# Three projection units opened by token halves at the norm borders, all norm sums in two banks, a fourth unit's weights in a home of their own

## The reference

```python
def rmsnorm(x, g):
    return x * rsqrt(mean(x * x) + EPS) * g

def swiglu(h, w_gu, w_down):
    gate, up = split(h @ w_gu, 2)
    return (silu(gate) * up) @ w_down

for l in range(2):
    h = rmsnorm(x, norm_pre[l, 0])
    x = x + 0.5 * rmsnorm(swiglu(h, ffn1_gu[l], ffn1_down[l]), norm_post[l, 0])
    h = rmsnorm(x, norm_pre[l, 1])
    mix = concat(attention, short_conv, recurrence)      # all from h @ w_in[l]
    x = x + rmsnorm(mix @ w_out[l], norm_post[l, 1])
    h = rmsnorm(x, norm_pre[l, 2])
    x = x + rmsnorm(memory_attention(h, mem[l]), norm_post[l, 2])
    h = rmsnorm(x, norm_pre[l, 3])
    x = x + 0.5 * rmsnorm(swiglu(h, ffn2_gu[l], ffn2_down[l]), norm_post[l, 3])
```

## Time and profile before

| | |
|---|---|
| median of 3 runs | 2857.54 us (2855.26 to 2858.48) |
| profiled execution | 2854.48 us |
| its span | 2852.7 us |
| TensorE matmul busy | 2767.0 us, 97% |
| VectorE busy | 1502.9 us, 53% |
| ScalarE busy | 1065.7 us, 37% |
| HBM traffic | 81 GB/s over the span |
| mean granted TensorE clock | 0.99 |

### The profile page before, as it was taken

How to read it: one execution, slowest core, us unless ns; L and a number is a source line. 1 busy time by engine, 2 the same in 40 slices (tenths; PEclk the granted TensorE clock), 3 DMA queues, 4 the chain that set the end, 5 groups by cost and what they waited for, 6 DMA issues and landing times.

```text
span 2852.7 us, 44015 instructions
## 1 busy us (share of the span) xinstructions
PE 2767.0 (97%) x18888; PEld 2578.0 (90%) x18888; DVE 1502.9 (53%) x2058; ACT 1065.7 (37%) x1567; POOL 107.1 (4%) x126
## 2 busy tenths in 40 slices
PE   8999999998999999999999999999989999999997
PEld 7999999997988889999989999999869888999996
DVE  5555326757563465552365552366576546555423
ACT  4333324325453343332243332242264434333322
POOL 0000000001100100000000000000001001000000
PEclk9999999999999999999999999999999999999998
DMA  3222332222233222322222322222223232222321
GB/s 109 85 81 81 91 87 61 68 73 81 89 98 101 70 67 81 87 87 82 77 74 81 88 86 82 77 75 60 76 78 104 89 89 67 82 85 84 88 82 63
DMA packets 420901, 233.07 MB, mean 82 GB/s; under 512 B 7124, under 2 KB 415736, under 8 KB 420760
## 3 DMA queue, kind: packets, MB, share of 16 engines
q1 hardware_dynamic: 414544, 210.33, 25.3%
q0 software_dynamic: 5984, 20.59, 2.2%
q10 hardware_dynamic: 232, 0.08, 0.0%
HBM read 219.44 MB, written 11.54 MB: 81 GB/s over the span
## 4 chain that ended last, share of the span: by engine, by line
PE 89%; DVE 7%; ACT 2%; DMA 1%; issue 1%; ACTq 0%; POOL 0%; DVEq 0%; POOLq 0%
PE PS L405 36%; PE PS L391 20%; PE PS L407 18%; PE PS L378 4%; PE PS L365 3%; PE PS L869 1%; DVE y_two L1461 1%; PE PS L587 1%; DVE x L1470 1%; PE PS L896 1%; DVE at_w L1774 1%; DVE h_two L1407 1%; DVE w_lo L1399 1%; DMA raw<-in_w_out_dram 1%; ACT w_hi L969 1%
## 5 line engine op out<-in xcount | busy, mean ns | idle before, releaser
L405 PE MATMUL PS<-h_two,w_hi 128*128 128x288 f32 (+2 forms) x4032 | 923.6, 337 | 4.4 <-DVE ut L1502 4.4
L1399 DVE TENSOR_TENSOR w_lo<-raw,w_hi 128x1024 fp32r<-128x1024 f32 (+1 forms) x372 | 489.2, 1315 | 648.1 <-ACT w_hi L969 645.6
L969 ACT ACTIVATE w_hi<-raw 128x1024 fp32r<-128x1024 f32 (+1 forms) x372 | 413.0, 1110 | 564.8 <-DMA raw<-in_ffn_down_dram 264.1
L405 PEld LDWEIGHTS PS<-h_two,w_hi 128*128 128x128 f32 x4032 | 605.7, 188 | 5.4 <-DVE ut L1502 5.1
L407 PE MATMUL PS<-h_two,w_lo 128*128 128x288 f32 x2688 | 571.4, 294 | 0.0
L407 PEld LDWEIGHTS PS<-h_two,w_lo 128*128 128x128 f32 x2688 | 471.5, 188 | 58.4
L405 PE MATMUL PS<-a_two,w_hi 128*128 128x288 f32 (+2 forms) x1848 | 422.8, 337 | 0.0
L391 PE MATMUL PS<-h_two,w_hi 128*128 128x288 f32 x2048 | 382.3, 300 | 0.0
L391 PEld LDWEIGHTS PS<-h_two,w_hi 128*128 128x128 f32 x2048 | 305.3, 189 | 4.9 <-issue 2.3
L405 PEld LDWEIGHTS PS<-a_two,w_hi 128*128 128x128 f32 x1848 | 277.5, 188 | 0.0
L407 PE MATMUL PS<-a_two,w_lo 128*128 128x288 f32 x1232 | 261.9, 294 | 0.0
(11 more groups left out here) (330 smaller groups left out, 3415.0 us busy)
## 6 DMA issues: line engine op xcount, KB each, us to landing
raw<-in_ffn_gu_dram SPq DMA_DIRECT2D x176, 512.0 KB, 3.8
raw<-in_ffn_down_dram SPq DMA_DIRECT2D x64, 704.0 KB, 4.5
raw<-in_w_in_dram SPq DMA_DIRECT2D x52, 512.0 KB, 3.9
raw<-in_w_out_dram SPq DMA_DIRECT2D x16, 512.0 KB, 3.7
raw<-in_w_mk_dram SPq DMA_DIRECT2D x16, 512.0 KB, 3.5
raw<-in_w_mv_dram SPq DMA_DIRECT2D x16, 512.0 KB, 3.6
raw<-in_w_mq_dram SPq DMA_DIRECT2D x16, 512.0 KB, 3.6
raw<-in_w_mo_dram SPq DMA_DIRECT2D x16, 512.0 KB, 3.6
```

The costliest lines, as they stand in the source:

```text
L405: mm(PW[slot][:, j, 0:c1 - c0], wt(ws)(0, k), row[:, c0:c1], start=begin, stop=end and j == 2, skip_group_check=True)
L969: A(whi(c % NW, slice(0, words)), rawu(c % NW, slice(0, words)), ACT.Copy).then_inc(whi_r, 1)
L1399: TT(wlo(c % NW, w_), rawu(c % NW, w_), f32(whi(c % NW, w_)), ALU.subtract).then_inc(wlo_r, 1)
```

## The change

**Opening.** Three units instead of two are opened by halves. Unit a by the first half with its pieces as before, then a + 1 and a + 2 by the first half; then the second halves interleaved: piece k of unit a, followed by piece k - 3 of a + 1 and of a + 2 (`lag = 3`). The FFN's whole units, and those of IN, begin at a + 3. At pn = 0 the third unit simply follows the second.

**Splits.** The split of e + 2 moves behind piece 10 on ScalarE (from 15) and behind piece 11 on VectorE (from the end of `update`). The split of e + 3 takes the place that e + 2 had on both. `pair(0)` has no split any more on either engine; a + 4's is still the first thing of `pair(1)`.

**A fourth home.** Unit a + 3 of F1, IN and F2 gets `raw4`, `w_hi4`, `w_lo4` (`slot_of`). Its load waits for the same count of finished units as the load of a + 2 (those up to a - 1). All other units keep slot u % 3, so a + 4 takes the slot of a + 1, whose end its load waits for.

**Banks.** Sums of the input norm go to `PX[1]` (but at pn = 2 and 6), beside those of the output norm; the opening's units lie in `S3`; the two wide tiles start at bank 0 and 3.

```diff
+FOURTH = [unit_base(0, phase) + 3 for phase in ("F1", "IN", "F2")]
+slot_of = lambda u: NW if u % UNITS in FOURTH else u % NW
+        S3 = [PX[0], PL[0], PL[1]]
-        PW = [PS[:, 2 + 3 * n:5 + 3 * n, :] for n in range(2)]
+        PW = [PS[:, 3 * n:3 * n + 3, :] for n in range(2)]
+        sums_of = lambda pn: PX[0] if pn % 4 == 2 else PX[1]
             def load(u, kt, src):
-                if u >= NW:
+                if slot_of(u) == NW:
+                    if u > NW:
+                        sp.wait_ge(unit_d, u - NW)
+                elif u >= NW:
                     sp.wait_ge(unit_d, u - NW + 1)
...
+                for n in (1, 2):
+                    pe.wait_ge(wlo_r, a + n + 1)
+                    if n == 2:
+                        pe.wait_ge(half_e, pn)
                     for k in range(KD):
+                        other(n, 0, k)
+                lag = 3
+                for k in range(KD + lag):
+                    if k < KD:
+                        m = pieces(a % NW, 0, 1, k, h_hi, h_lo, 0, k == 0, k == KD - 1, gate=upto(pn, 1, k))
+                    if k == lag:
                         pe.wait_ge(tile_e, t)
+                    if k >= lag:
+                        for n in (1, 2):
+                            m = other(n, 1, k - lag)
...
-                    9: lambda: pre_root(pn + 1, 0), 15: lambda: upcoming(e + 2),
-                    16: lambda: (raw_tile(proj[:, IN_PLACE[0], :] if pu == "F1" else sg, e, 0), pre_root(pn + 1, 1))})
+                    9: lambda: pre_root(pn + 1, 0), 10: lambda: upcoming(e + 2),
+                    16: lambda: (upcoming(e + 3), raw_tile(proj[:, IN_PLACE[0], :] if pu == "F1" else sg, e), pre_root(pn + 1, 1))})
...
-                update(pn, 0.5, {4: lambda: last_y(pn, 1), 6: lambda: upcoming(e + 1), 7: lambda: post_root(pn, 1)})
-                upcoming(e + 2)
+                update(pn, 0.5, {4: lambda: last_y(pn, 1), 6: lambda: upcoming(e + 1), 7: lambda: post_root(pn, 1), 11: lambda: upcoming(e + 2)})
+                upcoming(e + 3)
```

More of the change, by code:

```diff
@@ L106 @@
 NW = 3
+FOURTH = [unit_base(0, phase) + 3 for phase in ("F1", "IN", "F2")]
+slot_of = lambda u: NW if u % UNITS in FOURTH else u % NW
+loads_of = lambda u: sum(slot_of(v) == slot_of(u) for v in range(u + 1))
 HALF = [slice(0, HT), slice(HT, T)]
@@ L437, in close @@
                         for k in range(kt):
[L438 removed]
+                            m = pieces(u % NW, 2, h, k, hi, lo, k0, s == 0 and k == 0, s == len(units) - 1 and k == kt - 1)
                             if h == 1 and s == 0 and k == 0:
@@ L480, in opening, with other @@
                     return
+                def other(n, h, k):
+                    return pieces((a + n) % NW, n, h, k, h_hi, h_lo, 0, k == 0, k == KD - 1)
                 pe.wait_ge(tile_e, t - 1)
-                for h in range(2):
-                    for k in range(KD):
-                        m = pieces(a % NW, 0, h, k, h_hi, h_lo, 0, k == 0, k == KD - 1, gate=upto(pn, h, k))
-                        if h == 1 and k == KD - 1:
-                            m.then_inc(unit_d, 1)
[L487 to L496, removed]
-                        pe.wait_ge(tile_e, t)
[L498 to L501, removed]
+                for k in range(KD):
+                    pieces(a % NW, 0, 0, k, h_hi, h_lo, 0, k == 0, k == KD - 1, gate=upto(pn, 0, k))
+                    if k == 1:
+                        if (pn - 1) % 4 == 2:
+                            post_begin(pn - 1, 1)
+                        post_sum(pn - 1, 1)
+                    pre_sum(pn, 0, k)
@@ L505, in ffn @@
                 opening(pn, a, t)
[L506 to L512, removed]
+                pe.wait_ge(rs_r, 2 * pn + 1)
+                for n in range(3, 8):
+                    pe.wait_ge(tile_e, t + (n - 2 if n < 5 else n - 1))
+                    wide_unit(a + n, (n - 3) % 2, slot_of(a + n), h_two, middle={1: lambda: pre_sum_second(pn)} if pn and n == 3 else None)
+                with pe.Fori(0, (2 * KF - 8) // 6) as r:
+                    for n in range(8, 14):
+                        pe.wait_ge(tile_e, r * 6 + (t + n - 1))
+                        wide_unit(r * 6 + (a + n), (n - 3) % 2, (a + n) % NW, h_two)
                 b, t = unit_base(l, pd), tile_base(l, pd)
@@ L1064, in pair @@
                     A(a_hi[:, at, :], ut[:, :].rearrange("p (o t) -> p o t", o=1), ACT.Copy).then_inc(ahi_r, 1)
-                pair(0)
-                with act.Fori(0, 6) as r:
-                    for n in range(1, 4):
+                for n in range(4):
+                    pair(n)
+                with act.Fori(0, 5) as r:
+                    for n in range(4, 7):
                         pair(n, turn=r)
@@ L1512, in ffn @@
                     setup()
-                with v.Fori(0, 6) as r:
-                    for n in range(1, 4):
+                for n in range(1, 4):
+                    pair(n)
+                with v.Fori(0, 5) as r:
+                    for n in range(4, 7):
                         pair(n, turn=r)
```

147 lines of the change are left out of this document (81 added, 66 removed).

## The result

The changed kernel takes 2865.04 us, median of 10 runs (2860.38 to 2872.03), against 2856.72 (2850.69 to 2859.1, 10 runs) before: ratio 1.0034, 95% interval 1.0022 to 1.0046: slower by a third of a per cent. Forecast was 2864.5, by two new stops of TensorE at the borders and by the clock that falls behind them. Its profiled execution took 2865.35, span 2863.0.

What follows compares the result with a forecast made beforehand. TensorE, 89% of the span, was taken to bound the kernel. Borders +2.2, new low clock stretches +7.4, old ones gone -2.0 gave +7.6; less 0.6, 2857.5 + 7.0 = 2864.5 us, range 2857 to 2870.5.

Steps and rivals of the forecast that it cites:

- The first stop: At the five borders, TensorE waits 2.7 us for a+2's low part before a+2's first half.
- The second halves: In the openings, the three second halves take 9.50 us without a pause; pauses in front of pieces are gone.
- The second stop: In three FFN openings TensorE waits 2.6 us for a+4's split, queued behind the pair; in IN only 0.55.
- The sum without the clock: Three FFN borders +1.65, two IN borders +0.4, narrow matmuls +0.2: +2.2 us, between -1.2 and +5.6.
- The term of 0.05: Third unit as 48 narrow matmuls (6.34) instead of 40 wide ones (6.29) costs 0.05 us per FFN, four times.
- The 0.132 of a matmul: In a+1's first half, F1 of layer 1, a matmul costs 0.132 us, worked out from two trace rows.
- The clock: Behind eight pauses of 2.4 to 2.6 us, 5.3 low stretches at 1.4, +7.4; old ones gone, -2.0.
- rival A: Clock stays up behind the openings' stops; at most three low stretches, at most 2861, not measurable; chance 0.34.
- The bounds: Three low stretches in eight pauses and the small sum give 2857; all eight and the larger sum 2870.5.
- The step that explains the 3.06 us: Runs' median 3.06 above the profiled execution, likeliest from more low stretches, which the change removes too; 0.6 us off.
- B: At the borders a+2's low part is in time, five of eight pauses gone: -11.0 us, 2846.5; chance 0.04.

Runs made afterwards that it cites:

- e2: Changed kernel with a+2's split three pieces earlier on ScalarE and VectorE (first stop out); 2846.2 us, ratio 0.9978 to before.
- e5: The changed kernel run again, unaltered, on the chip of the next three runs; 2864.7 us, ratio 1.0043 to before.
- e3: Changed kernel with both splits moved, a+2's three pieces earlier and a+4's into pair(0) (both stops out); 2832.0 us, ratio 0.9931 to before.
- e1: Changed kernel with a+4's split moved in pair(0) ahead of SiLU on ScalarE and behind ut on VectorE (second stop out); 2855.0 us, ratio 1.0010 to before.
- e8: e3 with a+2's split behind piece 8 on ScalarE and behind 11 on VectorE, as the changed kernel has it there; 2852.9 us, ratio 1.0004 to before.
- e4: e3 without interleaving of the second halves (lag 8 instead of 3); 2838.4 us, ratio 0.9949 to before.
- e7: e3 with a+2's split behind piece 8 on ScalarE and behind 10 on VectorE (stop of 1.0); 2838.8 us, ratio 0.9955 to before.
- e9: e3 run again, the same kernel, on one chip with e10; 2828.7 us, ratio 0.9924 to before.
- e10: e4 run again, the same kernel without interleaving, on one chip with e9; 2835.8 us, ratio 0.9949 to before.
- e6: Kernel before with a+3's split moved in pair(0) ahead of SiLU on ScalarE and behind ut on VectorE; 2848.5 us, ratio 0.9986 to before.

## Why the prediction was right

**The first stop.** Predicted: a+2's first half at 1438.98 in the time of before. Measured: 1442.82 - 3.83 = 1438.99, VectorE waiting 0.76 for the high part where the working has 0.78. Taking it out (e2) is worth 57.44 against 61.68 at the border, less the one low stretch in the latter (1.54, below): 2.70, where 2.7 and 0.11 were predicted.

**The second halves.** 13.57 from a+2's start to the sum were predicted. With the clock up it is 13.66: in e5 from 1442.78 to 1456.44.

```profile
1442.78 0.40 PE L396 MATMUL PS<-h_two,w_hi 128*128 128x288 f32 x1 [2.55 <-DVE w_lo L1438]
...
1456.44 0.65 PE L447 MATMUL PS<-sqh,cst 128*128 128x288 f32 x2
```

**The second stop.** 8.57 from the sum to a+4 were predicted, 8.64 measured (1458.02 to 1466.66). Its price at the border is 57.44 - 54.83 = 2.61 (e2 against e3), where 2.6 and 0.11 were predicted. Both prices add up: 54.83 + 2.70 + 2.61 = 60.14, which is the changed kernel's 63.28 less two low stretches, 60.20.

**The sum without the clock.** An FFN border: 60.20 - 59.48 = 0.72, predicted 0.55. IN of layer 0: a+1's first half starts at 459.19, before at 459.16, and a+4 at 487.09; less 1.54 for one low stretch that is 0.16 later than before, predicted 0.08. The term of 0.05 for a third unit in narrow matmuls is too small to be seen: behind F1 of layer 0 the changed kernel is 0.03 later. The 0.132 of a matmul does not follow from the two rows that are named for it (3.25 us for 23 matmuls, the first of them slow), but the 13.66 us of the second halves bear it out.

**The clock.** The price was a little low: the stretch from a+2's start to the sum takes 15.20 with a low stretch (1442.82 to 1458.02) and 13.66 without, so 1.54, not 1.4. The count was low for this execution: seven, then five, for 5.3. In all executions with stops of 2.46 to 2.65 the clock fell behind 23 of 29 (the changed kernel 7 of 8, e5 5 of 8, e1 5 of 5, e2 2 of 3, e8 4 of 5). Where no stop over 1.2 stands in the openings of the third unit (e3, e4, e7, e9, e10), it fell behind none of 25. So rival A, for which these stops lie in work too dense for it, is wrong. The Trainium skill, page "TensorE: Matmul & The Clock Gate", section "Why this matters for your kernels", warns of idle gaps longer than any of these stops. Read as a length below which the clock stays up, as the prediction read it, that does not hold here: it fell behind 23 of 29.

With these numbers the opening terms of the profiled pair are 3 x 0.72 + 2 x 0.16 + 7 x 1.54 less 1.8 for the two low stretches of before (1.1 at IN of layer 1 and 0.7 at F2 of layer 0, each against the same border of the other layer), 11.5; with e5's five 8.4. The medians rose by 8.3, and by 11.9 in e5.

**What was luck.** The mechanism held, but that 2864.5 lies within 0.6 us of the median is luck. The chance of a fall was read from too few pauses: before's trace has eight pauses of 1.8 to 2.3 us in the attention and memory stages, not six. Two of 1.81 us, which end at 675.9 and 2078.5, are missing from the count, and behind both the clock stays up:

```profile
675.91 0.44 PE L727 MATMUL PS<-cst,at_w 128*128 128x128 f32 x2 [1.81 <-DVE at_w L1778]
```

```profile
675.90:679.20 3.30, 2.40 (x14) 1.00 0.00 0
2078.50:2081.80 3.30, 2.37 (x14) 1.00 0.01 2
```

With 4 of 8 the working gives four low stretches and 1.8 us less; 23 of 29 would have given 6.3. For the profiled pair it gave 7.6, and 10.9 was measured. The bounds, redone from the working's own terms, are 2857.9 and 2871.7 rather than 2857 and 2870.5; the result lies in both.

**What failed.** The step that explains the 3.06 us between the profiled execution and the median by more low stretches. It is one cause, and not the only one (last section), so the 0.6 taken off on it had no ground. Of the rivals, B's condition (a+2's low part in time) is what e2 sets up; B was priced at 11 us below the kernel before, e2 came out at 0.22% or 6.3. The openings of its profile come near the price: 9.9 us shorter than before, all five together. Its profiled execution is 8.8 below that of before, although two of its FFNs run at the longer of two paces (last section), 4.6 us; why the medians differ by only 6.3 is open.

**What stands behind the result.** The third unit by halves does what it is for: no piece of the second half is waited for. But each border pays both its gains back at the next thing that was late: the split of a+2, whose due time the third unit drew forward by 9 us, and the split of a+4, which nobody moved when the one ahead of `ut` was taken out. Moving these two splits on ScalarE and VectorE turns +0.4% into -0.7%. That the fourth home and the shared banks cost nothing was not tried by itself; at the five borders of e3 no wait of TensorE is put down to a load or to a bank.

## What to carry to other kernels

When an opening is widened, its weights fall due earlier: for every unit that is moved, write down when TensorE asks for it and what stands in front of its preparation on each engine, and move the preparation on all of them. A wait removed is worth what the next-latest operand leaves of it. And price a stop of some 2.5 us on TensorE at about half as much again, for the clock behind it.

## What the runs showed of the hardware

**The clock falls behind a single short stop.** After 2.5 us of idle time in otherwise full work the granted clock was 0.50 in 23 of 29 cases; after 1.03 us in none of five. The length alone does not decide: behind the pauses of 1.8 us in the attention stages of all twelve profiles a low stretch began within 3 us in 24 of 48. The old openings, with some three pauses of up to 0.5 in a row, had a low stretch in four of ten (before and e6), and no stop. The Trainium skill, page "TensorE: Matmul & The Clock Gate", section "A second HAM failure mode: psum-queue depth-cycling", tells of a kernel whose clock went to and fro for frequent short idles; those four agree.

**TensorE has two paces at the same granted clock.** In a whole FFN the wide units follow one another at one of two distances. F1 of layer 1, ScalarE's copies at the ends of two units that lie 30 units apart, before:

```profile
1492.34 0.65 ACT L977 ACTIVATE sq<-PS 128x576 f32<-128x576 f32 x1 [1.40 <-PE PS L407]
...
1681.14 0.65 ACT L977 ACTIVATE sq<-PS 128x576 f32<-128x576 f32 x1 [1.41 <-PE PS L407]
```

and in the changed kernel:

```profile
1500.20 0.65 ACT L1011 ACTIVATE sq<-PS 128x576 f32<-128x576 f32 x1 [1.25 <-PE PS L425]
...
1690.60 0.65 ACT L1011 ACTIVATE sq<-PS 128x576 f32<-128x576 f32 x1 [1.46 <-PE PS L425]
```

188.80 and 190.40: 6.293 or 6.347 a unit, 2.3 us over an FFN, with no idle time of TensorE between these rows and the clock at 1.00 in both. It isn't the change: e9 has 6.293 in this place, e3, the same program, 6.347. In 12 profiles F1 of layer 0 is at the longer distance eleven times, the other three FFNs 11 times in 36, and no FFN lies between. What chooses is open. It is a part of what sets two executions of one program apart, as e3's and e9's; another is TensorE's first wait, for a load, which takes 12.8 us in e3 and 9.5 in e9.
